# The causal mask of the first head's scores in wide attention rows: a VectorE addition in the place of a TensorE product

## The reference, cut to what matters

```python
m_s = (tok <= t[:, None])[:, :, None]
s_s = jnp.einsum('bqgrd,bgqkd->bgrqk', qr, k_sel).astype(jnp.float32) * scale
p_s = masked_softmax(s_s, m_s)
o_s = jnp.einsum('bgrqk,bgqkd->bqgrd', p_s.astype(v_sel.dtype), v_sel)
...
s_w = jnp.einsum('bqgrd,bkgd->bgrqk', qr, kwb).astype(jnp.float32) * scale
p_w = masked_softmax(s_w, m_w)
```

## Time and profile before

| | |
|---|---|
| median of 3 runs | 1270.26 us (1270.18 to 1270.35) |
| the profiled execution | 1270.12 us, of which the span of the trace is 1268.2 us |
| TensorE busy | 1247.5 us (98%) |
| VectorE, ScalarE, GpSimd busy | 763.0, 583.8, 405.1 us |
| the attention pairs | from about 147 to 318 us of the span |
| the wide stretches | about 163 to 212 us and 240 to 288 us |

### The profile page before, as it was taken

How to read it: one execution, slowest core, us unless ns; L and a number is a source line. 1 busy time by engine, 2 the same in 40 slices (tenths; PEclk the granted TensorE clock), 3 DMA queues, 4 the chain that set the end, 5 groups by cost and what they waited for, 6 DMA issues and landing times.

```text
span 1268.2 us, 19195 instructions
## 1 busy us (share of the span) xinstructions
PE 1247.5 (98%) x6742; PEld 1027.1 (81%) x6742; DVE 763.0 (60%) x1353; ACT 583.8 (46%) x1016; POOL 405.1 (32%) x270
## 2 busy tenths in 40 slices
PE   9999999999999999999999999999999999999997
PEld 7887877777888888888888888888878888888885
DVE  6844887675577877787874111111048848479487
ACT  6325476666544544455443222222366345254364
POOL 3433354545333333333333444444430110201200
PEclk9999999999999999999999999999999999999999
DMA  8533410000222222222222333333453061340601
GB/s 244 157 71 68 96 39 2 1 2 2 67 68 73 77 78 71 66 83 66 66 82 75 92 100 100 99 99 124 143 181 101 19 214 33 126 138 17 208 7 66
DMA packets 172312, 108.40 MB, mean 85 GB/s; under 512 B 25220, under 2 KB 163814, under 8 KB 172262
## 3 DMA queue, kind: packets, MB, share of 16 engines
q1 hardware_dynamic: 172022, 107.65, 29.1%
q10 hardware_dynamic: 240, 0.09, 0.0%
HBM read 104.84 MB, written 2.10 MB: 84 GB/s over the span
## 4 chain that ended last, share of the span: by engine, by line
PE 87%; DVE 4%; ACT 4%; issue 2%; POOL 1%; DMA 1%; SPq 1%; DVEq 0%; ACTq 0%; POOLq 0%
PE bank L2425 21%; PE bank L2047 17%; PE bank L2434 10%; PE bank L2051 9%; PE bank L2529 8%; PE bank L2534 4%; PE bank L2270 2%; PE bank L2444 2%; PE bank L2210 2%; PE bank L2249 2%; POOL prob L851 1%; PE bank L2107 1%; PE bank L2450 1%; PE bank L2405 1%; ACT prob L1002 1%
## 5 line engine op out<-in xcount | busy, mean ns | idle before, releaser
L834 POOL TENSOR_TENSOR wlo<-raw,whi 128x1024 fp32r<-128x1024 f32 x133 | 324.7, 2441 | 706.2 <-ACT whi L1080 388.7
L1080 ACT ACTIVATE whi<-raw 128x1024 fp32r<-128x1024 f32 x96 | 101.8, 1060 | 295.8 <-PE bank L2434 160.0
L2047 PE MATMUL bank<-h_hi,whi 128*128 128x512 f32 x488 | 194.4, 398 | 0.7 <-DVE h_lo L1324 0.7
L2047 PE MATMUL bank<-h_lo,whi 128*128 128x512 f32 x488 | 190.4, 390 | 0.0
L2425 PE MATMUL bank<-h_hi,whi 128*128 128x512 f32 x384 | 150.3, 391 | 1.3 <-DVE grp L1767 0.7
L2425 PE MATMUL bank<-h_lo,whi 128*128 128x512 f32 x384 | 149.4, 389 | 0.0
L2051 PE MATMUL bank<-h_hi,wlo 128*128 128x512 f32 x488 | 120.8, 390 | 0.0
L2047 PEld LDWEIGHTS bank<-h_hi,whi 128*128 128x128 f32 x488 | 91.8, 188 | 21.1 <-DVE h_lo L1324 2.5
L1855 DVE TENSOR_TENSOR mt<-bank,sig 128x512 f32<-128x512 f32 x16 | 11.1, 691 | 161.6 <-PE bank L2434 161.6
L1747 DVE SCALAR_TENSOR_TENSOR grp<-bank,vt,grp 128x511 f32<-128x511 f32 (+2 forms) x96 | 71.8, 748 | 59.1 <-ACT grp L1104 50.1
L2051 PEld LDWEIGHTS bank<-h_hi,wlo 128*128 128x128 f32 x488 | 91.6, 188 | 19.1
(11 more groups left out here) (318 smaller groups left out, 2503.6 us busy)
## 6 DMA issues: line engine op xcount, KB each, us to landing
raw<-in_w_in SPq DMA_DIRECT2D x75, 512.0 KB, 3.8
raw<-in_w_up SPq DMA_DIRECT2D x32, 512.0 KB, 4.1
draw<-in_w_down SPq DMA_DIRECT2D x16, 1024.0 KB, 6.3
raw<-in_w_ssm_branch SPq DMA_DIRECT2D x16, 512.0 KB, 3.7
raw<-in_w_in SPq DMA_DIRECT2D x20, 256.0 KB, 3.8
raw<-in_w_attn_branch SPq DMA_DIRECT2D x8, 512.0 KB, 3.6
raw<-in_w_o SPq DMA_DIRECT2D x8, 512.0 KB, 3.7
x_sb<-in_x SPq DMA_DIRECT2D x4, 512.0 KB, 5.2
```

What stands on the lines that cost most here:

```text
L834: nc.gpsimd.tensor_tensor(wlo[slot][:], raw[slot][:], whi[slot][:].bitcast(F32), ALU.subtract).then_inc(wlo_ready, units)
L1080: nc.scalar.activation(whi[slot][:], raw[slot][:], ACT.Copy).then_inc(whi_ready, 1)
L2047: T.matmul(bank[slot][:], whi[slot][:, k * P:(k + 1) * P], part[:, k, :], start=(k == 0 and n == 0), stop=False)
```

## The change

In wide pairs the first head's mask product (line 2214) is left out; its second score product raises `s_ready` instead. Before the maximum VectorE adds the f32 table (`cst[:, K_CB:K_CB + P]`, 0 and -1e30) to the 128 columns of the diagonal block in the score bank, in place, and waits for that addition. The second head and all narrow pairs keep their product.

```diff
@@ row_max(n), VectorE, the branch of wide pairs
                 else:
+                    causal = bank[b][:, pair(n)[1] * P:(pair(n)[1] + 1) * P]
+                    step(V.tensor_tensor(causal, causal, cst[:, K_CB:K_CB + P], ALU.add))
+                    step.wait()
                     V.tensor_reduce(nmax[:, at_step:at_step + 1], bank[b][:, 0:w], AX.X, ALU.max,
                                     negate=True).then_inc(max_ready, 1)
@@ scores(n), TensorE
                     for part in kk[br]:
-                        T.matmul(bank[b][:, off:off + w], q_hl[:, 2 * u + e, i * P:(i + 1) * P], part[:, g, 0:w],
+                        mm = T.matmul(bank[b][:, off:off + w], q_hl[:, 2 * u + e, i * P:(i + 1) * P], part[:, g, 0:w],
...
-                    if not narrow(n):
+                    if not narrow(n) and r2 == 0:
+                        mm.then_inc(s_ready, 1)
+                    elif not narrow(n):
                         T.matmul(bank[b][:, i * P:(i + 1) * P], ident_bf[:], causal_bf[:],
                                  start=False, stop=True, skip_group_check=True).then_inc(s_ready, 1)
```

More of the change, by code:

```diff
@@ L2209, in scores @@
                     for part in kk[br]:
-                        T.matmul(bank[b][:, off:off + w], q_hl[:, 2 * u + e, i * P:(i + 1) * P], part[:, g, 0:w],
-                                 start=(part is kk[br][0] and off == 0), stop=(part is kk[br][1]),
-                                 skip_group_check=narrow(n))
-                    if not narrow(n):
+                        mm = T.matmul(bank[b][:, off:off + w], q_hl[:, 2 * u + e, i * P:(i + 1) * P], part[:, g, 0:w],
+                                      start=(part is kk[br][0] and off == 0), stop=(part is kk[br][1]),
+                                      skip_group_check=narrow(n))
+                    if not narrow(n) and r2 == 0:
+                        mm.then_inc(s_ready, 1)
+                    elif not narrow(n):
                         T.matmul(bank[b][:, i * P:(i + 1) * P], ident_bf[:], causal_bf[:],
```

## The result

| | before | after |
|---|---|---|
| median | 1270.26 us (1270.00 to 1273.16, 11 runs) | 1274.68 us (1273.53 to 1276.22, 11 runs) |
| the profiled execution | 1270.12 us, span 1268.2 | 1274.68 us, span 1272.9 |
| its attention, from the start of the first score product to that of the last compressed product | 170.39 us | 175.10 us |

What follows compares the result with a forecast made beforehand. TensorE was taken to bound the kernel (busy 1247.5 of 1268.2 us), VectorE close behind in wide pairs; +2.5 us in the first stretch and +0.5 in the second made +3.0, forecast 1273.3 us, range 1270.4 to 1276.2.

Steps and rivals of the forecast that it cites:

- the sum: Both wide stretches of attention together: +3.0 us, from +2.5 in the first and +0.5 in the second.
- rival 4: VectorE sets the pace throughout, also in the second stretch's 16 pairs: +7.8 us, 1278.1; chance 0.18 with milder forms.
- the ledger: Account by turn in wide pairs: +0.33 us per addition where GpSimd releases late, -0.13 at other pairs, plus lacking slack.
- The cost of the addition: On VectorE, before each first maximum: 0.30 us plus 0.03 until the maximum starts, 0.33 us; bounds 0.21 and 0.57.
- Rival 2: Maximum starts 0.07 us before the addition's end, 0.22 us per addition: +0.7 us, 1271.0; chance 0.25 together with rival 3.
- The worth of the product: On TensorE, each of 32 mask products left out saves 0.13 us, 4.2 us of its time in all.
- the sign named for it: In wide pairs, first head's first score product to the second head's first: 0.46 us, not 0.60.
- The ledger of the first stretch: Turns 2, 5, 7, 9, 11 carry ten additions, +3.3 us; six other pairs gain 0.8; together +2.5.
- the criterion: Turns released by GpSimd with 0.35 us or less to spare lose 0.33 us per addition; other pairs gain 0.13.
- The second stretch: Turns 32 and 43 +1.3 us, twelve other pairs -1.6, lacking slack at 35, 37, 39: +0.5; sign: under 1 us longer.

Runs made afterwards that it cites:

- e8: Changed kernel plus six score-sized products in TensorE's wait before pair 1's compressed transposes; attention 3.61 us longer than before the change, ratio 1.0022.
- e10: The changed kernel unaltered, traced a second time; attention 3.53 us longer than before the change.
- e12: Second run of e8's kernel, on the same chip as a rerun of the changed kernel; 1273.80 us, ratio 1.0026, attention 3.48 us longer than before the change.
- e1: Kernel before, with the change only in the second wide stretch (pairs 32 to 47); attention 0.64 us longer, ratio 1.0006.
- e5: Changed kernel's additions in all wide pairs, but both mask products kept; attention 6.27 us longer than before the change, ratio 1.0039.
- e9: Kernel before without the first head's mask in wide pairs, no addition, six products filling TensorE's wait at pair 1; attention 1.80 us shorter, ratio 0.9981.

## Why the prediction was right, and where not

**Direction and size: right.** Without the fall of the clock three traces say +3.61, +3.53 and +3.48 us (e8, e10, e12; the last two with the 0.28 of pair 23 in their favour), the forecast +3.0. The fall adds 0.5 to 0.9 where it happens in the two traces of the changed kernel that have it. Of the 1.4 us between the median of 1274.7 and the forecast of 1273.3, 0.5 to 0.6 us belong to the sum and the rest goes with the fall. That the measured time lies inside the range in spite of a term that was missing is owed to the width that rival 4 gave it, and the sum came near in part by luck: see the ledger.

**The cost of the addition: right.** 0.29 us and 0.33 to the maximum. Rival 2 had the maximum 0.07 us ahead of the addition's end; in all 32 places it starts 0.034 to 0.035 us behind it. The Trainium skill, page "VectorE: DVE Perf Modes", section "The DRAIN you can't avoid", says for its chain that the semaphore costs nothing extra; here the instruction that waits starts some 0.10 us later than one that doesn't, and the measurement decides.

**The worth of the product: right per place, and right that it doesn't add up; the sign named for it wrong.** 0.11 to 0.14 us at each pair that TensorE paces. A pair's four score products and last mask, from the first start to that mask's start, took 165.33 - 164.19 = 1.14 us before (pair 3) and take 264.45 - 263.44 = 1.01 after (pair 39; both have 512 keys and the windowed branch): 0.13 less. But from the first head's first product to the second head's first it is 0.55 us in pair 39, where it was 0.59, and not the 0.46 that was named: of the pairs of 512 keys only 0 to 2 have 0.45. The larger part of the saving, 0.08 us, stands at the next product, which starts 0.24 us behind its predecessor and not 0.31.

```profile
263.44 1.17 PE L2213 MATMUL bank<-kw,q_hl 128*128 128x512 f32 x4
...
264.45 0.23 PE L2219 MATMUL bank<-causal_bf,ident_bf 128*128 128x128 bf16 x1
```

**The ledger of the first stretch: the sum near, partly by luck.** +2.5 forecast, +3.0 without the fall (e8, e12). Turns 5, 7, 9 and 11 step by 0.95, 0.58, 0.61 and 0.66 where 0.66 was taken, but each is followed by a step of -0.13 that the ledger had as nothing, since it let TensorE's saving be waited away: pairs 5 to 12 come to +2.3 us and not 2.6. What failed is the criterion: the pairs "released by GpSimd with 0.35 us or less to spare" were looked for, and pair 1 was entered as a gain of 0.13. It isn't released by GpSimd. TensorE waits there for ScalarE's copy of pair 0, which stands behind the exponential of pair 2 and so behind two additions. The step is +1.41 in after and +1.07 with the idle time filled, the largest of all. In return turn 2 steps by 0.04 and not 0.66 (e8), as the wait at pair 1 had given it slack. So 1.2 us were missed at pair 1 and 0.5 at pair 13, and nearly as much was taken too dear at turn 2 (0.6), in pairs 5 to 12 (0.4) and at pair 0 (0.3): the errors offset each other. Pair 13 (+0.36) was missed for a similar reason: its transposes stand behind scores of narrow pairs, and those wait for ScalarE's exponentials to free a bank. The waits show one such wait of TensorE in this stretch:

```profile
PEld bank L2213 <- ACT prob L1002: 0.3, 1, 0.3
```

**The second stretch: right.** Less than 1 us was named as the sign; the change has +0.69 from pair 29 to pair 47 (the scores of pairs 32 and 33 are issued at 30 and 31), e1 alone +0.64, forecast +0.5. Turns 32 and 43 step by 0.86 each (forecast 0.66), pairs 35, 37 and 39 together by +0.39, the rest by -0.13. Rival 4, VectorE setting the pace in all 16 pairs, is refuted: e5, with no product taken away, has +1.55 us in this stretch and not 5.3.

**The clock: not foreseen.** The term is missing from the sum. Rows of before showed TensorE idle for 1.28 us at this one place, the longest of its waits in attention, and both halves of the change lengthen it. The wait was there to be seen; that the clock would fall behind it was not, in the trace of before.

**How the parts stand together.** The products alone give -1.5 to -1.8 us (e9), the whole without a fall +3.5 to +3.6, so by difference of like traces the additions make +5.1 to +5.3; e5 alone had +6.27 with a fall. 32 x 0.33 = 10.6 us of VectorE's time thus came out as half of that on TensorE's way.

## What to carry to other kernels

Taking 0.13 us of work off the engine that is 98% busy and putting 0.33 us on one that is 60% busy, 32 times, lost time, because the second engine's loop (VectorE, ScalarE, VectorE, GpSimd) already ended just when TensorE wanted its result; read the slack between the two at every turn before moving anything, for every releaser and not for the likeliest one. Where an added instruction stands counts as much as how long it is: behind the first maximum the change cost about half of what it cost in front of it (1.72 us against about 3.5), as the other engine could start meanwhile. And ask of each lengthened wait of TensorE whether it is the longest in its surroundings, as it may cost the clock on top.

## What the runs showed of the hardware

A wait of TensorE of 2.0 to 2.7 us, in the midst of work at full clock, came in 5 of 7 traces with 3.4 us at a granted clock of 0.50, which began between 0.5 us before the end of the wait and 1.7 us behind it and cost 0.5 to 1.2 us; with six products of 512 columns issued into the wait (1.64 us) there was no fall at that place in 3 traces, and they cost nothing that shows. The fall depends on the execution as well as on the kernel: 2.65 us of idle time passed without one, and 1.99 us did not, and in e9 and e12 a fall came behind two waits of 0.9 us. An addition of 128 f32 columns from PSUM and back took 0.29 us, and a maximum that waits for it began 0.034 us behind its end. So one trace of such a kernel can be a microsecond off another of the same kernel, in the middle of the stretch that is being explained.
